# Forgetting attention: a second buffer for the transposed probabilities, and the previous pair attended two turns later

## The reference, cut to what matters

```python
def forgetting_attention(q, k, v, f_logit, f_bias):
    qf = q.astype(jnp.float32) * (HEAD_DIM ** -0.5)
    log_f = jax.nn.log_sigmoid(f_logit.astype(jnp.float32) + f_bias.astype(jnp.float32))
    c = jnp.cumsum(log_f, axis=1).transpose(0, 2, 1)

    def blk(i):
        ...
        mask = pos[None, :] <= tq[:, None]
        s = jnp.einsum('bqhd,bshd->bhqs', qb, kf) + cq[..., None] - c[:, :, None, :]
        p = jax.nn.softmax(jnp.where(mask, s, -jnp.inf), axis=-1)
        return jnp.einsum('bhqs,bshd->bqhd', p, vf)
```

## Time and profile before

| | |
|---|---|
| median of three runs | 1997.96 us (1995.35 to 2005.08) |
| the profiled execution | 1994.73 us, span 1993.1 us |
| granted TensorE clock, mean | 0.988 of full speed |
| TensorE matmuls busy | 1919.5 us, 96% of the span |
| VectorE, ScalarE, GpSimd busy | 1193.3, 772.7, 573.4 us |
| the stage of the change | from 823.79 us to 903.85 us of the span, where the next projection starts |

### The profile page before, as it was taken

The page is one execution under the profiler, slowest core; times in us unless marked ns, Lnnn a source line. Parts: engine busy times, 40 slices in busy tenths (PEclk is TensorE's granted clock), DMA queues, the critical chain, the costliest instruction groups (busy, mean ns, idle before and its releaser), DMA issues.

```text
span 1993.1 us, 25599 instructions
## 1 busy us (share of the span) xinstructions
PE 1919.5 (96%) x9666; PEld 1553.0 (78%) x9666; DVE 1193.3 (60%) x2013; ACT 772.7 (39%) x1304; POOL 573.4 (29%) x427
## 2 busy tenths in 40 slices
PE   9998999999999999989999999989989999999997
PEld 7876568888888888757988888878838778888876
DVE  4567757742762632375772376364458689667676
ACT  4245643321331232572432233254434254434432
POOL 1223623100000200480310011043440457777740
PEclk9999999999999999999999999999999999999999
DMA  7321033642442222102463255212210322333344
GB/s 284 98 88 43 1 127 119 221 146 98 156 168 106 84 99 93 65 2 106 159 211 116 95 175 198 92 57 74 96 42 1 106 85 106 106 127 110 122 148 148
DMA packets 39387, 223.26 MB, mean 112 GB/s; under 512 B 5936, under 2 KB 6256, under 8 KB 18928
## 3 DMA queue, kind: packets, MB, share of 16 engines
q1 hardware_dynamic: 27616, 179.99, 25.0%
q0 software_dynamic: 11664, 41.80, 6.4%
HBM read 217.64 MB, written 2.10 MB: 110 GB/s over the span
## 4 chain that ended last, share of the span: by engine, by line
PE 78%; DVE 14%; DMA 2%; POOL 2%; issue 2%; ACT 2%; SPq 0%; DVEq 0%; POOLq 0%; ACTq 0%
PE G L412 35%; PE G L2411 7%; PE G L2310 6%; PE TR L2411 4%; PE OB L2411 4%; PE TR L412 2%; PE OB L412 2%; PE G L1549 2%; PE G L2331 2%; PE OB L1502 1%; POOL weights_low L438 1%; PE TR L2310 1%; DVE stat_sb L2890 1%; PE OB L2310 1%; PE OB L1549 1%
## 5 line engine op out<-in xcount | busy, mean ns | idle before, releaser
L432 ACT ACTIVATE weights_high<-ring_sb 128x1024 fp32r<-128x1024 f32 (+1 forms) x312 | 321.8, 1037 | 419.4 <-PE OB L2411 134.2
L438 DVE TENSOR_TENSOR weights_low<-ring_sb,weights_high 128x1024 fp32r<-128x1024 f32 x204 | 251.4, 1236 | 382.8 <-ACT weights_high L432 382.7
L412 PE MATMUL G<-xt_high,weights_high 128*128 128x512 f32 (+2 forms) x1256 | 460.4, 367 | 5.6 <-DVE xt_low L1257 2.1
L412 PE MATMUL G<-xt_high,weights_low 128*128 128x512 f32 (+2 forms) x1256 | 458.0, 365 | 0.0
L412 PE MATMUL G<-xt_low,weights_high 128*128 128x512 f32 (+2 forms) x1256 | 457.8, 364 | 0.0
L438 POOL TENSOR_TENSOR weights_low<-ring_sb,weights_high 128x1024 fp32r<-128x1024 f32 (+1 forms) x108 | 268.2, 2497 | 380.3 <-ACT weights_high L432 325.6
L412 PEld LDWEIGHTS G<-xt_high,weights_high 128*128 128x128 f32 (+1 forms) x1256 | 233.7, 186 | 46.5 <-issue 5.8
L412 PEld LDWEIGHTS G<-xt_high,weights_low 128*128 128x128 f32 (+1 forms) x1256 | 233.7, 186 | 38.6
L412 PEld LDWEIGHTS G<-xt_low,weights_high 128*128 128x128 f32 (+1 forms) x1256 | 233.8, 186 | 37.8
L2200 POOL DMA_DIRECT2D KS_sb<-ada x64 | 33.9, 530 | 475.5 <-DVE og_sb L2762 475.5
L2039 DVE SCALAR_TENSOR_TENSOR KS_sb<-G,cols_sb,KS_sb 128x441 f32<-128x441 f32 (+2 forms) x160 | 109.5, 684 | 65.1 <-ACT KS_sb L1779 65.1
(11 more groups left out here) (496 smaller groups left out, 3656.0 us busy)
## 6 DMA issues: line engine op xcount, KB each, us to landing
ring_sb<-chunks SPq DMA_DIRECT2D x155, 1024.0 KB, 4.8
KS_sb<-ada POOLq DMA_DIRECT2D x64, 512.0 KB, 4.6
ring_sb<-slabs SPq DMA_DIRECT2D x2, 2048.0 KB, 7.6
wide_sb<-x_features SPq DMA_DIRECT2D x4, 512.0 KB, 8.8
X_sb<-slabs SPq DMA_DIRECT2D x1, 2048.0 KB, 14.1
rows_sb<-ln_gain POOLq DMA_DIRECT2D x4, 512.0 KB, 5.2
rows_sb<-ln_bias POOLq DMA_DIRECT2D x4, 512.0 KB, 6.4
X_sb<-x SPq DMA_DIRECT2D x4, 512.0 KB, 9.5
```

The lines of the kernel that those rows point to most:

```text
L412: mm = nc.tensor.matmul(out, lhsT=a, rhs=b, start=(3 * i + j == 0), stop=(3 * i + j == n - 1))
L432: nc.scalar.activation(Wh[:, n % 4, c], raw_quarter(Q)[:, c], ACT.Copy).then_inc(w_hi, 1)
L438: tt_(out=Wl[:, n % 4, c], in0=raw_quarter(Q)[:, c], in1=Wh[:, n % 4, c], op=ALU.subtract).then_inc(w_lo, 1)
```

## The change

The three tensors PT, qb and kb become one, PL, at the same place and of the same size, with the old names as views of it. Pairs of even n now keep their transposed probabilities in PL, pairs of odd n in PTU as before. With two buffers, A(n-1) can stand behind T0(n) and T1(n) in TensorE's program, and it is put there. On VectorE, M(n-1) moves from behind C1(n) to behind C3(n). No instruction is added or removed, and no DMA is touched.

```diff
         wide = sb("wide", [P, 32, S])
         SC = sb("SC", [P, 2, TT, S])
-        PT = sb("PT", [P, TT, S])
-        qb = sb("qb", [P, 2, S])
-        kb = sb("kb", [P, 2, S])
+        PL = sb("PL", [P, 8, S])
+        PT, qb, kb = PL[:, 0:4, :], PL[:, 4:6, :], PL[:, 6:8, :]
@@
+        PTF2 = [PL[:, :, :].rearrange("p (u b) n -> p u b n", u=2), PTU]
+
         def staged(n):
@@
-                        mm = nc.tensor.matmul(OB[n % 2][e * HD:(e + 1) * HD, b * P:S], lhsT=V[:, b, c:c + HD], rhs=PTU[:, e, b, b * P:S],
+                        mm = nc.tensor.matmul(OB[n % 2][e * HD:(e + 1) * HD, b * P:S], lhsT=V[:, b, c:c + HD], rhs=PTF2[n % 2][:, e, b, b * P:S],
                                               start=(b == 0), stop=(b == 3))
@@
             for n in range(N_FOX):
                 scores(n + 1, 0)
                 scores(n + 1, 1)
-                attended(n - 1)
                 turn(n, 0)
                 turn(n, 1)
+                attended(n - 1)
                 scores(n + 1, 2)
@@
-                nc.vector.tensor_copy(PTU[:, es[0]:es[-1] + 1, 0:t + 1, t * P:(t + 1) * P], ps).then_inc(pair_copied, 1)
+                nc.vector.tensor_copy(PTF2[n % 2][:, es[0]:es[-1] + 1, 0:t + 1, t * P:(t + 1) * P], ps).then_inc(pair_copied, 1)
@@
                 copy(n, 0)
                 copy(n, 1)
-                mixed_low(n - 1)
                 least(n + 1, 2)
                 invert(n + 1, 0)
                 copy(n, 2)
                 copy(n, 3)
+                mixed_low(n - 1)
                 least(n + 1, 3)
```

## The result

The changed kernel takes 2001.54 us (median of 20 runs, 1998.93 to 2012.18) against 1998.15 us for the kernel before (20 runs, 1991.15 to 2006.02). The medians are 3.4 us apart. The ratio on record is 1.0023 with a 95% interval of 1.0012 to 1.0034, which is slower by 4.6 us, and by 2.4 to 6.8 us with the interval. It is not the plain quotient of the two medians, which would be 1.0017; nor are the ratios further down. The forecast was 2002.9 us, slower by 4.9.

The account below looks back on a forecast made before the run. All four engines are nearly full, so the longest closed circle of waits sets the period, 9.80 us instead of 8.98. Start +1.32, six periods +4.89, end -1.33: +4.9 on the 1997.96 us median gives 2002.9, range 1996 to 2009.

Parts of the forecast that it names:

- circle two: Closed circle of waits from A through ScalarE and GpSimd to T1 and the next A: 9.80 us, for pairs up to 7.
- circle one: Closed circle of waits from A through VectorE, then GpSimd's P1 and T1, to the next A: 9.78 us a period.
- the hand-offs: Delays between engines within the sums, taken as 0.1 us each, with 0.05 and 0.17 for the range.
- The low end of the range: Length of the longer closed circle with the shortest delays between engines: 9.65 us, in a range up to 10.0.
- Start and end: First A of the stage comes 1.32 us later; the stretch from seventh to eighth A gets 1.33 us shorter.
- Waits: Per period: T1 about 1 us for GpSimd, K some 1.8, H some 0.5 for A, VectorE some 2.5 at L2.
- At the new place as at the old: On VectorE, M's 0.60 us was claimed to lie in circle one both before and after its move.
- called itself wrong: Signs of error: A 9 us apart or less, T1 not waiting for GpSimd, or the periods' granted clock under 1.00.
- one stretch at the end of the stage: Between the last two A before the change, TensorE idled 1.8 of 7.12 us and the clock held; cited against clock falls.
- the rival: TensorE's clock falls in each of six periods, 1.5 us each: 8.9 us more, 2011.8 us in all; chance 0.07.
- the 85 forecast: Predicted length in us of the changed stage, which took 80 us before.

Follow-up runs that it names:

- the cuts: Changed kernel with I1 moved beside I0: 9.75 to 9.76 us periods at full clock; with G moved ahead: 9.79 to 9.80; both moves: 9.11 to 9.15, ratio 0.9991.
- the best order tried: Changed kernel with A between T0 and T1, M behind C5, I0 and I1 ahead of C0, G ahead of scaling: periods 8.40 or 8.41 us, ratio 0.9979.

## Why the prediction was right, point by point

- **The period.** Forecast 9.80 us by circle two and 9.78 by circle one; measured 9.78 to 9.80 undisturbed. Both circles are shown: by the added instruction (10.35 with a K, 9.78 without), and by the cuts, of which one alone changes next to nothing and both give 0.67 us. Which one binds was left open; it is circle one, by 0.03 us. That the sums hit the period to 0.01 us is partly luck, since circle two came out 0.04 us shorter than its sum, and the hand-offs were taken at 0.1 us on the strength of two rows. The low end of the range has a slip that changes nothing: with 0.05 us in place of each 0.1 the longer circle is 9.70 us, not 9.65.
- **Start and end.** Forecast +1.32 and -1.33 us; measured: the first A comes 16.59 us into the stage (851.34 less 834.75) instead of 15.23 (839.02 less 823.79), +1.36, and the last stretch is 5.76 instead of 7.12, -1.36. With six periods of 9.79 us, undisturbed, the path comes to +4.8 us, where the forecast was +4.9.
- **Waits.** T1 behind GpSimd 0.83 us (forecast about 1), K 1.82 (1.8), H 0.47 (0.5), L2 2.50 (2.5).
- **The copies and A.** A's wait of 0.53 us went, as forecast, and was less than what took its place.
- **M.** That M costs nothing by waiting held, and at its new place its 0.60 us lies in circle one. "At the new place as at the old" did not hold: with M in its old place circle one is 9.54 us (the sixth period of that run) and not 9.78, as part of M there ran beside S2. Circle two, 9.74 us in that run, hides this in the other five. That M's old place was the better one in the old order too (0.3 us a period) the prediction didn't say.
- **The clock.** Here the prediction was off, and by its own sign: it called itself wrong if the clock of the periods was under 1.00. It gave the falls a chance of 0.07 and reasoned from one stretch at the end of the stage, where TensorE had been idle for longer and the clock had held. Two falls came in each of two profiled executions, at 1.6 us each (forecast 1.5). The step that failed is the inference from one stretch that held to a whole chain of periods. Even that stretch doesn't always hold: with the two buffers alone its clock was 0.81. What the rival said would happen in all six periods happened over four, as two falls. Of the rule that was cited, from the Trainium skill, "TensorE: Matmul & The Clock Gate", section "A second HAM failure mode: psum-queue depth-cycling", the trace bears out that the clock goes back and forth under short idle times, but in two places over six periods.
- **The total.** With the falls the stage of the two profiled executions took 88.1 and 88.3 us, and not the 85 forecast: 8.1 and 8.2 more than before. That is more than the interval of the timed runs allows (2.4 to 6.8 us); the 4.8 us without falls lies inside it. Whether fewer falls came in the timed runs, or time was made good elsewhere, no run here shows. So the mechanism of the slower periods is shown, but that the whole time came out so near the forecast is in part luck.
- **Elsewhere.** The profiled execution after took 2010.80 us and that of before 1994.73, 16 us apart. 11.0 us of it is there before the stage begins (834.75 against 823.79), in code that the change does not touch; 8.1 us is the stage, and behind the stage the changed kernel was 3.0 us faster (1086.2 us against 1089.3), again without a change of the code. A stretch from before the stage:

```profile
150.00:300.00 150.00, 134.99 (x815) 89.96 (x814) 101.94 (x325) 81.25 (x216) 59.86 (x62) 0.89 0.14 52
```

The same stretch of the kernel before had a clock of 0.95, and the second execution of the changed kernel reached the stage at 825.7. Only stages may be compared between two profiles here, not spans.

## What to carry to other kernels

Before an instruction is moved behind another engine's product, write down the closed circle that it then lies in, one period long, with durations from one period of the trace; all circles through the new wait must be summed, since cutting one of two nearly equal ones gives nearly nothing. An engine that is busy 95% of a period may have no weight and one that gets its turn in a new circle has all of it: an added instruction of known length on that engine tells which. And the second buffer was worth less here than the wait of 0.53 us a period that it was to remove: the best order tried got 0.22 us out of it, while reordering small steps around the old buffer got 0.36. The clock has to be watched beside the circles: the order that lost 4.8 us by its waits lost another 3.3 us by two falls in the profiled executions.

## What was not expected of the hardware

The granted clock fell in the same periods of two executions of the changed kernel that reached the stage at different times, 834.75 and 825.7 us, and in partly different periods of two executions of the kernel with I1 moved. The two falls of the changed kernel's first execution began at 860.5 and 901.5 us, within 0.2 us of the end of TensorE's wait of 0.83 us at T1; in the periods between them it waited just as long at T1, was busy 8.77 of 9.79 us, and the clock held.

Neither the share of busy time nor the longest gap foretells a fall. With A behind T1 and M in its old place TensorE was busy less (8.53 of 9.74 us) and waited longer at T1:

```profile
858.78 0.44 PE L587 MATMUL TR<-table_sb,SC_sb 128*128 128x128 f32 x2 [1.03 <-POOL ring_sb L738]
```

Yet the clock stayed at 1.00 in all six periods. And at 5.3 of 7.1 us busy, after a gap of 1.76 us, it held in the kernel before and fell to a mean of 0.81 with the two buffers alone, after the same gap and in the same order of work. What does decide it, no run here shows.
